# The row sums of 64 tokens on VectorE instead of TensorE, and every fourth lower half of a split on GpSimd

## What is computed

```python
u = u_tab[eidx]
v = v_tab[eidx]
a = jax.nn.gelu(jnp.einsum('thkd,td->thk', u, ht))
return jnp.einsum('thk,thkd->td', g * a, v)
```

## Time and profile before

| | |
|---|---|
| runs | 2587.07, 2589.88, 2590.89 us; median 2589.88 us |
| the profiled execution, by the same clock as the runs | 2589.13 us |
| its span from the first to the last instruction | 2587.4 us |
| mean granted TensorE clock | 0.952 of full speed |
| busy share of the span | PE 90%, DVE 61%, ACT 34%, POOL 33% |

### The profile page before, as it was taken

How to read it: one execution, slowest core, us unless ns; L and a number is a source line. 1 busy time by engine, 2 the same in 40 slices (tenths; PEclk the granted TensorE clock), 3 DMA queues, 4 the chain that set the end, 5 groups by cost and what they waited for, 6 DMA issues and landing times.

```text
span 2587.4 us, 32955 instructions
## 1 busy us (share of the span) xinstructions
PE 2334.6 (90%) x13072; PEld 1790.2 (69%) x13072; DVE 1586.1 (61%) x3185; ACT 869.6 (34%) x1617; POOL 850.6 (33%) x648
## 2 busy tenths in 40 slices
PE   8999988997987777779899966799999999999999
PEld 7756555675544444368677865688888888888887
DVE  5358567453100000054537989699889888889986
ACT  3134333432000000033424348544433333333332
POOL 0013221001110010000004548365567776666760
PEclk9999898998999999969998967899999999999999
DMA  5345010246999999842005117999999999999993
GB/s 192 126 173 195 33 66 33 101 182 236 427 426 426 426 426 426 339 164 98 33 33 204 41 47 246 359 409 342 349 406 413 414 413 413 382 403 399 400 396 126
DMA packets 141711, 693.69 MB, mean 268 GB/s; under 512 B 18428, under 2 KB 45092, under 8 KB 107760
## 3 DMA queue, kind: packets, MB, share of 16 engines
q1 hardware_dynamic: 80816, 479.68, 46.6%
q0 software_dynamic: 60736, 211.85, 21.0%
HBM read 659.52 MB, written 38.81 MB: 270 GB/s over the span
## 4 chain that ended last, share of the span: by engine, by line
PE 64%; DVE 17%; DMA 15%; ACT 2%; issue 1%; SPq 0%; DVEq 0%; POOLq 0%; ACTq 0%
PE psum L3606 14%; DMA arena<-w 13%; PE psum L3571 12%; PE psum L2236 4%; PE psum L470 4%; PE psum L986 4%; PE psum L1707 3%; PE psum L3577 2%; DVE arena L3821 2%; PE psum L3575 2%; PE psum L1287 2%; PE psum L1302 2%; DVE rounded L3704 2%; PE psum L2387 2%; DVE arena L3291 1%; PE psum L3529 1%
## 5 line engine op out<-in xcount | busy, mean ns | idle before, releaser
L3606 PEld LDWEIGHTS psum<-rounded,rounded 128*128 128x128 f32 x2880 | 432.0, 189 | 29.9 <-ACT rounded L3653 11.7
L3606 PE MATMUL psum<-rounded,rounded 128*128 128x320 f32 x2880 | 445.0, 311 | 7.1 <-DVE rounded L3704 6.2
L3571 PE MATMUL psum<-rounded,rounded 128*128 128x512 f32 x1536 | 398.7, 396 | 2.7 <-DVE rounded L3724 2.3
L3517 POOL DMA_INDIRECT arena<-u_rows,arena x192 | 283.5, 1476 | 180.0 <-DVE arena L3821 57.2
L3571 PEld LDWEIGHTS psum<-rounded,rounded 128*128 128x128 f32 x1536 | 283.4, 189 | 80.0 <-issue 14.3
L3517 POOL DMA_INDIRECT arena<-v_rows,arena x192 | 288.6, 1503 | 152.4 <-DVE arena L3832 66.8
L3704 DVE TENSOR_TENSOR rounded<-arena,rounded 128x1024 fp32r<-128x1024 f32 x248 | 303.0, 1222 | 6.6 <-ACT rounded L3639 6.6
L1707 PE MATMUL psum<-arena 128*64 128x256 f32 x2048 | 234.5, 384 | 59.5 <-DMA arena<-w 58.8
L1835 DVE COPY arena<-psum 128x256 f32<-128x256 f32 x32 | 13.6, 425 | 407.3 <-PE psum L1774 407.3
L3639 ACT ACTIVATE rounded<-arena 128x1024 fp32r<-128x1024 f32 x248 | 260.0, 1049 | 8.6 <-DMA arena<-uv 7.7
L1707 PEld LDWEIGHTS psum<-arena 128*64 128x64 f32 x2048 | 148.7, 138 | 156.4 <-DMA arena<-w 63.1
(11 more groups left out here) (515 smaller groups left out, 3782.6 us busy)
## 6 DMA issues: line engine op xcount, KB each, us to landing
arena<-w SPq DMA_DIRECT2D x96, 2048.0 KB, 42.4
arena<-uv SPq DMA_DIRECT2D x124, 1024.0 KB
arena<-wada SPq DMA_DIRECT2D x12, 2048.0 KB
gd<-arena SPq DMA_DIRECT2D x19, 1024.0 KB, 9.3
arena<-gd SPq DMA_DIRECT2D x30, 640.0 KB
arena<-wp SPq DMA_DIRECT2D x8, 2048.0 KB
arena<-win SPq DMA_DIRECT2D x4, 2048.0 KB
arena<-wq SPq DMA_DIRECT2D x4, 2048.0 KB
```

Of the source, the lines that this page charges most:

```text
L3517: po.indirect_dma_start(out=ROWS_OF[i % len(ROWS_OF)], out_offset=None, in_=src, in_offset=bass.IndirectOffsetOnAxis(ap=column.bitcast(U32 ...
L3571: ins = pe.matmul(PS[:, 2 * n + half, :], gg[:, z, 128 * n:128 * n + 128], v[:, y, 512 * half:512 * half + 512], x == 0 and i == 0, x == 1 ...
L3606: ins = pe.matmul(PS[:, 7, 0:DT], w[:, y, k, :], hv[:, z, :], k == 0 and i == 0, k == 7 and i == 2)
```

## The change

- TensorE's 32 rounds are gone, with the transposed index, the weight matrices `W32`, the transposed weights `WT`, and ScalarE's copy of bank 6.
- In their place VectorE has 64 operations "few sum", for k = 0 to 63 at unit 63 + 175k/64: `H2T2 = row * weight + H2T2` on 128x1024. Their rows come through the same number of gathers (64 sets of `v_rows`), by the index `IDX2`.
- `fold_few` adds the two halves by eight matmuls with the matrix `BOTH` where it had four transposes.
- The lower half of the split of every fourth unit (j = 16, 20, ..., 236, 56 units) is made by GpSimd in its own list, between its gathers, in place of VectorE. TensorE and the SP queue wait for whichever engine makes it.
- GpSimd's list is cut into steps, one for each unit: in step j first the split of unit j + 3, if it is GpSimd's, and then the gathers whose buffers are freed by operations of units before j.

```diff
-    ROUND = {63 + 175 * r // 31: r for r in range(ROUNDS)}
+        FEW_SUMS.setdefault(63 + 175 * k // FEW, []).append(k)
...
+    def by_pool(j):
+        return j % 4 == 0 and 16 <= j < 240
+    def split_done(j):
+        return E.po["split", j] if by_pool(j) else E.dv["split", j]
...
         def piece(c):
-            sp.wait_ge(*E.dv["split", 2 * (c - 3) + 1])
+            if c > 3:
+                sp.wait_ge(*split_done(2 * (c - 3)))
+            sp.wait_ge(*split_done(2 * (c - 3) + 1))
...
+        def split(j):
+            s = SPL[j % 5]
+            po.wait_ge(*E.ac["split", j])
+            po.tensor_tensor(s[:, 1024:2048], at(RAW[(j // 2) % 3] + 1024 * (j % 2), 1024), s[:, 0:1024].bitcast(F32),
+                             ALU.subtract).then_inc(*E.po("split", j))
+        for i in range(len(ROWS_OF)):
+            gather(i)
+        i = len(ROWS_OF)
+        for j in range(len(UNITS)):
+            if j + AHEAD < len(UNITS) and by_pool(j + AHEAD):
+                split(j + AHEAD)
+            while i < len(ROWS_IN_TURN) and ROWS_IN_TURN[i - len(ROWS_OF)][2] < j:
+                gather(i)
+                i += 1
...
-            if j in ROUND:
-                gather_round(ROUND[j])
...
         for j, (kind, x) in enumerate(UNITS):
-            if j + AHEAD < len(UNITS):
+            if j + AHEAD < len(UNITS) and not by_pool(j + AHEAD):
                 split(j + AHEAD)
...
+            for k in FEW_SUMS.get(j, []):
+                row, there = rows_of("few sum", k)
+                dv.wait_ge(*there)
+                if k:
+                    dv.wait_ge(*E.dv["few sum", k - 1])
+                    dv.scalar_tensor_tensor(H2T2, row, Z2[:, k:k + 1], H2T2, ALU.mult, ALU.add).then_inc(*E.dv("few sum", k))
...
         def fold_few():
-            pe.wait_ge(*E.ac["few sum"])
-            for k in range(4):
-                ins = pe.transpose(PS[:, 6, 128 * k:128 * k + 128], H2T2[:, 128 * k:128 * k + 128], IDENT)
+            pe.wait_ge(*E.dv["few sum", FEW - 1])
+            for k in range(8):
+                ins = pe.matmul(PS[:, 6, 64 * k:64 * k + 64], H2T2[:, 128 * k:128 * k + 128], BOTH, True, True)
```

More of the change, by code:

```diff
@@ L2685, in build @@
     IDX = at(o, 128); o += 128
-    IDXT = at(o, 64); o += 64
     PXS2 = at(o, SMALL_T); o += SMALL_T
@@ L2988, in build @@
     slots = [o]; o += GG_W
-    W32 = [at3(o + 64 * i, 2, 32) for i in range(4)]; o += 256
     assert o <= 2 * O_TEMP
@@ L3352, in gather_po @@
                     pick(n, *IPARTS[PICK.index(step)])
-    E = Stage(counter, "dense", "pe ac dv")
+    E = Stage(counter, "dense", "pe ac dv po")
     d_out = dma_counter("out")
@@ L3377, in build @@
     for j in range(len(UNITS)):
-        ROWS_IN_TURN += [("few dot", k, 0) for k in FEW_DOTS.get(j, [])]
-        ROWS_IN_TURN += [("dot", k, 0) for k in DOTS.get(j, [])]
-        ROWS_IN_TURN += [("sum", k, 0) for k in SUMS.get(j, [])]
-        if j in ROUND:
-            ROWS_IN_TURN += [("round", ROUND[j], c) for c in range(2)]
-    ROW_NO = {x: i for i, x in enumerate(ROWS_IN_TURN)}
+        ROWS_IN_TURN += [("few dot", k, j) for k in FEW_DOTS.get(j, [])]
+        ROWS_IN_TURN += [("dot", k, j) for k in DOTS.get(j, [])]
+        ROWS_IN_TURN += [("sum", k, j) for k in SUMS.get(j, [])]
+        ROWS_IN_TURN += [("few sum", k, j) for k in FEW_SUMS.get(j, [])]
+    ROW_NO = {(x, k): i for i, (x, k, j) in enumerate(ROWS_IN_TURN)}
     def unit(kind, x):
         return UNITS.index((kind, x))
+    def by_pool(j):
+        return j % 4 == 0 and 16 <= j < 240
+    def split_done(j):
+        return E.po["split", j] if by_pool(j) else E.dv["split", j]
     def rows_of(*x):
@@ L3495, in dense_po, with gather @@
         po.wait_ge(*E.pe["rows"])
-        for i, (kind, k, c) in enumerate(ROWS_IN_TURN):
+        def gather(i):
+            kind, k, _ = ROWS_IN_TURN[i]
             if i < len(ROWS_OF) and QUARTER_OF[i]:
@@ L3505, in dense_po @@
                 was, before, _ = ROWS_IN_TURN[i - len(ROWS_OF)]
-                po.wait_ge(*(E.pe["round", before] if was == "round" else E.dv[was, before]))
+                po.wait_ge(*E.dv[was, before])
             if (kind, k) == ("dot", 0):
@@ L3519, in dense_po @@
                 *d_rows[i % len(ROWS_OF)]("row", i))
-    def dense_pe(pe):
[L3522 to L3531, removed]
+        def split(j):
[12 more added lines that the diff above has]
+                i += 1
+        assert i == len(ROWS_IN_TURN)
+    def dense_pe(pe):
         def rows_of_hidden(name):
@@ L3593, in dense_pe @@
         for j, (kind, x) in enumerate(LOOP):
-            pe.wait_ge(*E.dv["split", j])
+            pe.wait_ge(*split_done(j))
             if j == 2:
@@ L3620, in dense_pe @@
             for x in TAIL:
-                pe.wait_ge(*E.dv["split", unit("v", x)])
+                pe.wait_ge(*split_done(unit("v", x)))
                 pe.wait_ge(*E.dv["gg", x])
@@ L3688, in dense_ac @@
                 ac.activation(Z2 if few else ZS, Z2 if few else ZS, ACT.Gelu_apprx_tanh).then_inc(*E.ac("z", WEIGHTS[j]))
[L3689 to L3692, removed]
         ac.wait_ge(*E.dv["sum", REST - 1])
+        ac.wait_ge(*E.dv["few sum", FEW - 1])
         for n in (0, 2, 1):
@@ L3817, in dense_dv @@
             for k in FEW_DOTS.get(j, []):
-                row, there = rows_of("few dot", k, 0)
+                row, there = rows_of("few dot", k)
                 dv.wait_ge(*E.ac["few rows"])
@@ L3822, in dense_dv @@
             for k in DOTS.get(j, []):
-                row, there = rows_of("dot", k, 0)
+                row, there = rows_of("dot", k)
                 dv.wait_ge(*E.ac["rows"])
@@ L3827, in dense_dv @@
             for k in SUMS.get(j, []):
-                row, there = rows_of("sum", k, 0)
+                row, there = rows_of("sum", k)
                 dv.wait_ge(*there)
@@ L3835, in dense_dv @@
                     dv.tensor_scalar(H2T, row, ZS[:, 0:1], None, ALU.mult).then_inc(*E.dv("sum", 0))
+            for k in FEW_SUMS.get(j, []):
[4 more added lines that the diff above has]
+                    dv.scalar_tensor_tensor(H2T2, row, Z2[:, k:k + 1], H2T2, ALU.mult, ALU.add).then_inc(*E.dv("few sum", k))
+                else:
+                    dv.wait_ge(*E.dv["w", "few"])
+                    dv.tensor_scalar(H2T2, row, Z2[:, 0:1], None, ALU.mult).then_inc(*E.dv("few sum", 0))
             if j in WEIGHTS:
@@ L3860, in dense_dv @@
                     c = 128 * (k % 4)
-                    src = PS[:, 6, c + 64 * (k // 4):c + 64 * (k // 4) + 64] if few else PS[:, 6 + k // 4, c:c + 128]
+                    src = PS[:, 6, 64 * k:64 * k + 64] if few else PS[:, 6 + k // 4, c:c + 128]
                     dst = X[:, k, DT:DT + FEW] if few else X[:, k, DT + FEW:T]
```

34 lines of the change are left out of this document (4 added, 30 removed).

## The result

The change takes 2636.78 us (median of 4 runs, 2634.40 to 2643.16) against 2590.39 us (median of 4, 2587.07 to 2591.44): 46 us or 1.77% slower, ratio 1.0177 with the interval 1.0159 to 1.0194. 2657 us was forecast with a range of 2617 to 2700. The profiled execution took 2637.9 us, 48.8 more than that of before.

The account below looks back on a forecast made before the run. TensorE, full from 1703 us on, was taken to bound the kernel, VectorE after the change. Units 16 to 47 gave +7, 63 to 147 +28, 148 to 239 +32, ends +1: +68 us on 2589.9, so 2657 us, range 2617 to 2700.

Parts of the forecast that it names:

- TensorE's bound and what rounds cost: Dense stage: TensorE full, 14.40 us a group of four units without rounds; a round costs 1.20 us, all 32 cost 38.
- VectorE becomes the bound: Dense stage: VectorE needs 16.05, 16.17 and 15.27 us a group, more than TensorE's 14.40 everywhere.
- rival 2: Dense stage: GpSimd sets the pace, its gathers staying long, 17.7 us a group; 2713 us, halfway 2683; chance 0.12.
- 2.1 us of VectorE's time for a split on GpSimd: Dense loop: operations reading SBUF exclude each other, so each GpSimd split holds VectorE 2.1 us, bounds 0 and 2.4.
- Rival 1: Dense stage: VectorE and GpSimd hardly hinder each other, a split costing under about 1.05 us; 2563 us; chance 0.08.
- it is on time as long as GpSimd keeps up: GpSimd's list: its split for unit j + 3, in step j, comes on time for TensorE and the SP queue; nothing added.
- rival 3: Dense stage: loss and saving balance, about 1.05 us a split, as GpSimd's splits fall into VectorE's gaps; 2590 us; chance 0.04.
- rival 4: TensorE's clock drops, being busy only 88%; at 0.93 a group takes 15.5 us, still under 16.4; no chance given.
- The group before: Units 63 to 147 and 148 to 239 before the change: a group of four units takes 15.06 and 15.09 us.
- VectorE's gaps: Groups with few sums: 2% (0.33 us) of idle time added to VectorE, giving 16.38 and 16.50 us a group.
- VectorE's work: Units 63 to 147 and 148 to 239: VectorE needs 16.05 and 16.17 us a group, few sums adding 1.87.
- the 0.16 of W32: VectorE loses the 32 operations of 0.219 us for W32, 0.16 us less a group of four units.

Follow-up runs that it names:

- e_tiny: The change, but GpSimd subtracts only the first 8 of the 1024 columns of each of its 56 lower halves, every wait kept; 2565.62 us.
- e_twice: The change, with each of GpSimd's 56 subtractions made twice, the second behind a wait for the first; 2756.25 us.
- e_writes: The change, but GpSimd fills its 56 lower halves with zeros by three writes, some 2.5 us in all, and reads nothing; 2567.95 us.
- e_sums_only: The change without its GpSimd part: few sums on VectorE, no rounds, all lower halves on VectorE; 2581.37 us.
- e_eighth: The change with every eighth lower half on GpSimd in place of every fourth (28 in place of 56); 2611.04 us.

## Why the prediction was right, step by step

**TensorE's bound and what rounds cost.** Right. A round-free group takes 14.40 us where TensorE is free to run (units 48 to 62: 50.39 us for 14 units).

The sum didn't use the price, though. 32 rounds of 1.20 us over 44.5 groups (units 62 to 240) are 0.86 us a group, as measured (15.29 and 15.24 less 14.40); the forecast wrote a saving of 0.66 to 0.69, which comes to 30 us and not its own 38.

**VectorE becomes the bound.** Right: 99% busy, and TensorE waits for lower halves, from 1690 to 2600 us 36.3 us for VectorE's and 18.9 for GpSimd's. So the sign that would have spoken for rival 2 (TensorE waits mainly for GpSimd while VectorE idles for rows) didn't appear. TensorE was busy for 92 to 93%, not 87 to 90.

**2.1 us of VectorE's time for a split on GpSimd.** Right, measured 2.19 (e_tiny) and 2.13 (e_twice, where some waits of TensorE are in it). The longest operations are longer than forecast: a split 3.44 us, a dot 3.79 and a sum 3.96 where 3.3 was expected, and GpSimd's 4.34 where it was 3.5. Both directions of holding, read from two places of the trace before, are at work at once: GpSimd waits for the operation that runs, and the next one waits for GpSimd.

**The rivals.** Rival 1's edge was 1.05 us a split, and 2.19 were measured. That case made real, e_tiny, gave 2566 us where 2563 was worked out. The nearness is partly luck: in units 62 to 148 the group went from 15.29 to 14.83 us, not from 15.06 to 14.57, so two errors cancelled. GpSimd's pace (rival 2) was no bound: e_writes has as long a list and took 2568 us, and a gather takes 1.42 and 1.56 us on average in the change, much as before. But "it is on time as long as GpSimd keeps up" was too simple: the first lower half was 2.76 us late, and 8.7 us of waits came in the middle of e_writes. The gaps of rival 3 vanished as VectorE became late: 1.3% and 1.0% of the windows were left. The clock of rival 4 hardly fell: 0.99 in both long parts.

**Where the forecast was some 20 us too high.** The sum gave +68 us, the profiled executions differ by 48.8. The mechanism was right and three sizes in units 62 to 240 were off, all to the same side (units 16 to 48 grew by 4.4 us in place of 7, and TensorE's wait of 2.8 us at unit 16 stood in no term):

- *The group before.* I divided the window 1876:2196 by 85 units. It holds 84, and the window 2196:2543 holds some 91 and not 92, since unit 240 starts only at 2547.87. By the starts of the units, a group took 15.29 and 15.24 us, not 15.06 and 15.09. That is 21.5 x 0.23 + 23 x 0.15 = 8 us too much growth. A count of one operation in a window is a poor way to find its units: cut at the starts.
- *VectorE's gaps.* I added 2% or 0.33 us; the gaps are 346.10 - 341.64 = 4.5 us and 373.78 - 370.13 = 3.7 us, 0.21 and 0.16 a group: 7 us.
- *VectorE's work.* 16.05 and 16.17 us a group were forecast with the hold, 15.89 and 16.09 measured: 5 us. Inside, two errors partly cancel. The miscounted unit also made VectorE's base too small, 13.37 and 13.49 where it was 13.55 (291.27/21.5) and 13.68 (314.72/23). And the few sums cost 1.39 and 1.43 us a group (e_sums_only: 14.78 and 14.95 busy, less the base, plus the 0.16 of W32), not 1.87. At least in part this is overlap: on a full VectorE an operation starts some 0.08 us before the last one ends (at 2072.35 and 2072.43 us above), so a duration is more than an operation's share of the time. That this is all of the difference isn't shown.

**Where the change's own saving went.** TensorE gave back its 38 us, but VectorE, 1.6 to 1.7 us a group behind it, took on 1.2 and had its gaps as well, so the few sums alone are worth 9 us (e_sums_only). Moving the splits, which frees VectorE of about 1.0 us a group (14.78 and 14.95 busy in e_sums_only, 13.83 and 13.82 in e_tiny) and holds it for 2.2, then took 2636.78 - 2581.37 = 55 us.

## What to carry to other kernels

Before an operation is moved from VectorE to GpSimd, look at what VectorE does meanwhile: if its operations read two operands from SBUF and the GpSimd one reads SBUF as well, they take turns, and most of GpSimd's longer time is paid by VectorE (here 2.1 to 2.2 us for an operation of 2.40 us, to be rid of one of about 1.1). The move does little harm only while VectorE has that much room. Here a dot with one operand in PSUM, and a GpSimd operation that only writes, were free of it. Look too at where the moved operation stands in the new engine's list: behind a run of gathers the first one came 2.76 us late, in e_eighth 8.30. When the bound passes from one engine to another that is nearly as full, the worth of a change is the distance between the two, not the time that was removed.

## What the hardware showed beyond that

In no slice of the dense stage, in any of these kernels, did the transfers go over 414 GB/s (409 and 411 in e_tiny's two windows), where rival 1's price took the 426 of another stage as the limit. Whether 414 is a limit isn't shown. And TensorE's granted clock, 1.00 while it was full, was 0.92 in e_twice's window above, where it was busy for 338.60 of 396.40 us: a mixture of its two levels, 2.4 and 1.2 GHz. VectorE, busy for 395.42 of 396.40 us, set the pace there, so the lower clock can have cost little.
